# A two-layer decoder kernel: tile 1's last four heads sorted and chosen in two windows, and the order around the first gathered rows

## The reference

```python
q = (xc @ w_query).reshape(c, PEER_HEADS, 2, half)
scores = jnp.einsum('chpd,hpnd->chpn', q, sub_keys, preferred_element_type=jnp.float32)
s1, i1 = lax.top_k(scores[:, :, 0], PEER_TOPK)
s2, i2 = lax.top_k(scores[:, :, 1], PEER_TOPK)
cand_s = (s1[..., :, None] + s2[..., None, :]).reshape(c, PEER_HEADS, PEER_TOPK * PEER_TOPK)
cand_id = (i1[..., :, None] * PEER_NKEYS + i2[..., None, :]).reshape(c, PEER_HEADS, PEER_TOPK * PEER_TOPK)
top_s, top_j = lax.top_k(cand_s, PEER_TOPK)
ids = jnp.take_along_axis(cand_id, top_j, axis=-1)
gate = jax.nn.softmax(top_s, axis=-1)
u = expert_u[ids]
pre = jnp.einsum('chkd,cd->chk', u, xc, preferred_element_type=jnp.float32)
act = gate * jax.nn.gelu(pre, approximate=False)
return jnp.einsum('chk,chkd->cd', act.astype(expert_v.dtype), expert_v[ids])
```

## Time and profile before

| | us |
|---|---|
| median of three runs | 1544.27 |
| lowest, highest | 1544.26, 1545.46 |
| the profiled execution | 1546.54 |
| its span | 1544.8 |
| busy PE / DVE / ACT / POOL | 1133.4 / 1043.4 / 577.2 / 583.4 |
| bytes moved by DMA | 607.35 MB, mean 393 GB/s |

### The profile page before, as it was taken

How to read it: one execution, slowest core, us unless ns; L and a number is a source line. 1 busy time by engine, 2 the same in 40 slices (tenths; PEclk the granted TensorE clock), 3 DMA queues, 4 the chain that set the end, 5 groups by cost and what they waited for, 6 DMA issues and landing times.

```text
span 1544.8 us, 18402 instructions
## 1 busy us (share of the span) xinstructions
PE 1133.4 (73%) x6396; PEld 450.3 (29%) x6396; DVE 1043.4 (68%) x2678; ACT 577.2 (37%) x1802; POOL 583.4 (38%) x516
## 2 busy tenths in 40 slices
PE   8887776986568865778657887699566867666666
PEld 6653232451113522234112443245011311111112
DVE  3677987579996246667998537767799565454545
ACT  0415447333334145423334325733234343333332
POOL 0024444334544332434544333443444353333430
PEclk9999888897779967888687997899577986676668
DMA  9278999999999999999999999999999999999993
GB/s 360 99 317 366 412 408 376 386 408 418 421 420 411 418 417 419 420 405 396 421 421 407 417 418 421 395 398 417 420 421 420 369 422 422 421 421 422 421 421 156
DMA packets 90253, 607.35 MB, mean 393 GB/s; under 512 B 9904, under 2 KB 10416, under 8 KB 24624
## 3 DMA queue, kind: packets, MB, share of 16 engines
q0 software_dynamic: 73728, 536.90, 84.5%
q1 hardware_dynamic: 16272, 69.02, 11.2%
q10 hardware_dynamic: 160, 0.26, 0.1%
HBM read 605.09 MB, written 1.05 MB: 392 GB/s over the span
## 4 chain that ended last, share of the span: by engine, by line
DMA 35%; PE 27%; DVE 26%; ACT 5%; issue 5%; POOL 2%; SPq 0%; POOLq 0%; ACTq 0%; DVEq 0%
DMA ring<-in_rows,ids 34%; DVE ring L1314 12%; PE acc L578 10%; PE bank L902 3%; PE bank L981 2%; POOL ring L545 2%; PE bank L611 2%; PE bank L741 2%; PE bank L616 1%; DVE wb L1651 1%; PE bank L646 1%; DVE top_i L1645 1%; DVE y L1724 1%; DVE top_i L1660 1%; ACT diag L1071 1%
## 5 line engine op out<-in xcount | busy, mean ns | idle before, releaser
L545 POOL DMA_INDIRECT ring<-in_rows,ids x512 | 583.2, 1139 | 923.5 <-PE acc L578 758.6
L578 PE MATMUL acc<-ring,diag 64*64 64x512 f32 x3968 | 671.5, 786 | 311.4 <-ACT diag L1071 307.5
L1314 DVE CUSTOM_DVE_ANT_0 ring<-ring,xc 128x1024 f32<-128x1024 f32 x504 | 608.4, 1224 | 380.3 <-DMA ring<-in_rows,ids 369.7
L1062 ACT ACTIVATE gel<-pre 128x1 f32<-128x1 f32 x512 | 103.4, 202 | 782.4 <-DVE pre L1314 746.9
L578 PEld LDWEIGHTS acc<-ring,diag 64*64 64x64 f32 x3968 | 139.9, 160 | 782.4 <-ACT diag L1071 662.1
L1071 ACT ACTIVATE diag<-cst,act_w 128x64 f32<-128x64 f32 x512 | 178.1, 348 | 16.7
L1068 ACT ACTIVATE act_w<-gate,gel 128x1 f32<-128x1 f32 x512 | 150.7, 294 | 16.7
L902 PEld LDWEIGHTS bank<-hT,held 128*128 128x128 f32 x384 | 43.8, 192 | 10.9 <-issue 8.1
L902 PE MATMUL bank<-hT,held 128*128 128x128 f32 x384 | 46.1, 278 | 1.0 <-DVE hT L1353 1.0
L741 PE MATMUL bank<-wring,hT 128*128 128x512 f32 x96 | 44.2, 603 | 3.1 <-DVE hT L1356 3.1
L1314 DVE DVE_READ_ACCUMULATOR2_ANT pre<- 128x1 f32 x512 | 42.1, 82 | 0.0
(11 more groups left out here) (285 smaller groups left out, 1073.9 us busy)
## 6 DMA issues: line engine op xcount, KB each, us to landing
wring<-in_w_in SPq DMA_DIRECT2D x16, 978.0 KB
wring<-in_w_out SPq DMA_DIRECT2D x12, 1024.0 KB
wring<-in_w_gate SPq DMA_DIRECT2D x11, 1024.0 KB
held<-in_w_query SPq DMA_DIRECT2D x8, 1024.0 KB, 22.0
ring<-in_rows,ids POOLq DMA_INDIRECT x512
ring<-in_w_in SPq DMA_DIRECT2D x8, 978.0 KB, 15.7
held<-in_w_out SPq DMA_DIRECT2D x2, 1024.0 KB, 12.3
held_latent<-in_w_latent SPq DMA_DIRECT2D x2, 768.0 KB
```

The costliest lines, as they stand in the source:

```text
L545: pool.indirect_dma_start(out=ring[:, n % RING, :], out_offset=None, in_=rows, in_offset=bass.IndirectOffsetOnAxis(ap=index, axis=0),).the ...
L578: last = pe.matmul(acc[rows_of(c), r, :], diag[rows_of(r), j, :], ring[rows_of(r), j, D:][:, cols_of(c)], start=False, stop=True, skip_gro ...
L1062: act.activation(gel[:, j:j + 1], pre[:, j:j + 1], ACT.Gelu).then_inc(gelued, 1)
L1314: dve.tensor_tensor_reduce(out=u, in0=u, in1=x, scale=1.0, scalar=0.0, op0=ALU.mult, op1=ALU.add, accum_out=pre[:, j:j + 1]).then_inc(dott ...
```

## The change

It does five things.

1. SP issues slab 0 of `w_in` right behind x, ahead of the constants.
2. In tile 0's `rest`, `copy_group(1)` stands behind the squares and the reciprocal root.
3. `FIRST` is 1; `query_group(2)` stands two turns later in `choose(0, 1)`, and `keys_group(2)` with ACT's copy of the queries moves into `leave(1)`.
4. In window 0, chunks 2 and 3 of tile 1 (its heads 4 to 7) are only sorted, in two turns each. The sum of the window's numbers is 159.4 instead of 177.8. The other four turns of each chunk (`pick`) stand in window 1, in `front(2)`, between the eight input slabs. Window 1's own numbers are as they were.
5. Tile 1's gate is made in two halves: heads 0 to 3 in window 0, heads 4 to 7 in window 1. SP's load of `held_latent` waits for `latent_done`, no longer for `ids_ready`.

```diff
-FIRST = 3
+FIRST = 1
+NEAR = 2
...
 def window_turns(w):
 
     turns = HEAD + LATE_LEAVE + CHOOSE * 3 if w == 0 else EMBED
+    if w == 0:
+        return turns + HOPS_LATE + REST + CHOOSE * NEAR + CHOOSE[0:2] * (len(CHUNKS[1]) - NEAR) + [2]
...
             for c in range(len(CHUNKS[w + 1])):
-                parts["choose"](w + 1, c, turn)
+                if w == 0 and c >= NEAR:
+                    parts["sort"](w + 1, c, turn)
+                else:
+                    parts["choose"](w + 1, c, turn)
...
             load(h[:, 0, :], x[0:P, :], x_in[0])
+            load(ring[:, 0, 0:IN_W], w_in[0, 0:P, :], slab_in[0])
             load(cst[:], consts, consts_in)
...
                 turn()
+                if s == 1:
+                    keys_group(2)
                 next_of(normed)
...
                 for i in range(len(CHOOSE)):
-                    if (s, i) == (0, 1):
-                        if c == 2:
-                            next_of(latT_ready)
-                            next_of(cum_copied)
-                        if 1 <= c <= 3:
-                            query_group(c + 1, 0, KT // 4)
-                    if (s, i) == (0, 2) and 1 <= c <= 3:
-                        query_group(c + 1, KT // 4)
-                    if (s, i) == (0, 4) and 1 <= c <= 3:
+                    if (s, c, i) == (0, 2, 0):
+                        next_of(latT_ready)
+                        next_of(cum_copied)
+                    if s == 0 and 1 <= c <= 3:
+                        first = 3 if c == 1 else 1
+                        if i in (first, first + 1):
+                            query_group(c + 1, (i - first) * KT // 4, (i - first + 1) * KT // 4)
+                    if (s, i) == (0, 4) and 2 <= c <= 3:
                         keys_group(c + 1)
...
             def front(s, turn):
-                for _ in FRONT:
+                for n in range(len(FRONT)):
+                    if s == TILES and n in (4, 8):
+                        gate_exps(1, NEAR + n // 4 - 1)
                     turn()
...
                 copy_hT(gn[:, l, G_MIX:G_MIX + KT])
+                if s == TILES:
+                    for c in range(NEAR, len(CHUNKS[1])):
+                        pick(1, c, turn)
+                    return
...
                 if s == 0:
-                    copy_group(1, l)
                     next_of(group_in, 2)
                     for i in range(2):
                         squares(y[:, i * 256:(i + 1) * 256], i, wa[:, 512:768], 256)
                     rsqrt(2)
+                    copy_group(1, l)
                     next_of(row_gain_in, 16)
                     add_out(0, 0)
```

More of the change, by code:

```diff
@@ L121, in gate_heads, with gates_until @@
         return slice(*CHUNKS[s][c])
-    return slice(0, PH) if c == len(CHUNKS[s]) - 1 else None
+    if s == 1 and c == NEAR - 1:
+        return slice(0, CHUNKS[s][c][1])
+    if c == len(CHUNKS[s]) - 1:
+        return slice(CHUNKS[s][NEAR][0] if s == 1 else 0, PH)
+    return None
+def gates_until(s, k):
+    parts = [(i, gate_heads(i, c)) for i in range(STEPS) for c in range(len(CHUNKS[i]))]
+    ends = [(i, part.stop * TOPK) for i, part in parts if part]
+    return min(n + 1 for n, (i, end) in enumerate(ends) if i == s and end >= k)
 class Shares:
@@ L458, in _ @@
             load(posi[:], pos, small_in)
-            for k in range(KT):
+            for k in range(1, KT):
                 load(ring[:, k, 0:IN_W], w_in[0, k * P:(k + 1) * P, :], slab_in[k])
@@ L947, in choose, with sort @@
                         release(products(0, 1, weights(), bank[2:4]))
+                    turn()
+            def sort(s, c, turn):
+                for _ in range(2):
                     turn()
@@ L1048, in tail @@
                 totals(bank[0][:, 3:4], [slice(1, 2), slice(2, 3)], 5)
-            walk(Stream(experts, 2), {"front": front, "leave": leave, "rest": rest, "choose": choose, "embed": embed, "lift": lift,
+            walk(Stream(experts, 2), {"front": front, "leave": leave, "rest": rest, "choose": choose, "sort": sort, "embed": embed, "lift": lift,
                                        "begin": begin, "finish": lambda t: None, "ahead": ahead, "tail": tail})
@@ L1075, in __call__ @@
                     if b > a:
-                        act.wait_ge(gate_ready, len(CHUNKS[0]) + step if step else min(c + 1 for c, part in enumerate(CHUNKS[0]) if part[1] * TOPK >= b))
+                        act.wait_ge(gate_ready, gates_until(step, b))
                     Stream.__call__(self, step, a, b)
@@ L1129, in leave @@
                     act.wait_ge(slab_used, KT)
+                    copy_query(2)
                 turn()
@@ L1235, in choose, with gate_exps, sort @@
                                        ACT.Copy).then_inc(lift_copied, 1)
+            def gate_exps(s, c):
+                next_of(gate_in)
+                hs = gate_heads(s, c)
+                if hs:
+                    if (s, c) == (0, 0):
+                        next_of(scale_ready)
+                    act.activation(best_v[:, hs], best_v[:, hs], ACT.Exp,
+                                   scale=ffn_r[:, s % 2:s % 2 + 1]).then_inc(gate_exp, 1)
+            def sort(s, c, turn):
+                for _ in range(2):
+                    turn()
             def begin(w):
@@ L1289, in tail @@
                     act.dma_start(out[P:P + HALF_P, cols_of(c)], result_tail[rows_of(c), 0, :]).then_inc(stored, 16)
-            walk(GatedStream(experts, 1, first=FIRST), {"front": front, "leave": leave, "rest": rest, "choose": choose, "embed": embed, "lift": lift,
+            walk(GatedStream(experts, 1, first=FIRST), {"front": front, "leave": leave, "rest": rest, "choose": choose, "sort": sort, "embed": embed, "lift": lift,
                           "begin": begin, "finish": lambda t: None, "ahead": ahead, "tail": tail})
@@ L1675, in keys_next8, with sort, pick @@
                 next8(range(2 * a, 2 * z), top_v, top_i, lambda i: score(i, s), spare, s == 0)
+            def sort(s, c, turn):
+                keys_top8(s, c)
+                turn()
+                keys_next8(s, c)
+                turn()
             def choose(s, c, turn):
+                sort(s, c, turn)
+                pick(s, c, turn)
+            def pick(s, c, turn):
                 l, t = layer_tile(s)
```

18 lines of the change are left out of this document (4 added, 14 removed).

## The result

The changed kernel took 1532.95 us (median of six runs, 1530.67 to 1536.55) beside 1543.86 us for the kernel before on the same chip. The ratio is 0.9932, with a 95% interval of 0.9916 to 0.9948. A second set of six runs on another occasion gave 1531.10 us beside 1541.45, a ratio of 0.9919 (0.9894 to 0.9945). So the gain is 10.4 to 10.9 us by the medians, 10.5 to 12.5 by the ratios, where the forecast took off 14.2 us.

A forecast was written before the change was run, and what follows sets the result against it. Bound: bytes at full DMA rate plus holes where DMA moves less. Terms 0.8 + 2.0 + 4.8 + 1.2 + 5.4 = 14.2 us off 1544.3 gave 1530.1 us; own range 1527 to 1533.5, 8-in-10 range 1525 to 1539.

The forecast's parts named there:

- Slab 0 ahead: First projection: slab 0 issued ahead of the constants lets the third slab be used sooner; gain 0.8 us, ends 0 and 1.6.
- cannot overtake: Start loads: engines consume descriptors in ring order, so the constants queue behind slab 0, putting `gn` at 8.0 us.
- The copy: Tile 0's rest: copy_group(1) behind the root removes PE's 2.02 us wait for DVE's `y`; gain 2.0 us, low end 1.0.
- The restart: At 120 us: the ninth gather goes out at about 111.8, closing the 4.8 us hole; low end 2.5.
- the wait only moves: Rival: `leave(1)` waits for a late query copy and could reopen the whole 4.8 us; 1534.9 us, 12%.
- The hole at 190: Window 0: DMA sets the pace up to turn 27, so the 1.2 us hole closes; low end 0.
- `rest(1)`: Window 0: more rows per turn close the holes at 230, 240, 250 and 340; gain 5.4 us, ends 0 and 8.5.
- one more gather under way closes each: Step for 230, 240, 250 and 340: each hole, 1.0 to 2.0 us, is less than one row.
- The picks in window 1: Between tile 2's slabs: 17.8 us of DVE picks fill its waits for rows; cost 0, bad end 3 us.
- The slower rival: DVE becomes the bound between the slabs, adding picks, gate and ACT work; +7.3 us, 1551.6 us, 5%.
- Its dearer form: Counting a drain with each table load, 2.66 us per table switch, DVE bounding between slabs costs about 2.8 us more.
- the small holes stay: Rival: window 0's small holes could be fixed stalls as more rows load ACT too; gain 8.8 us less forecast, 1535.5 us, 23%.

The follow-up runs named there:

- slab_undone: The changed kernel with slab 0 of the input projection behind the constants again; one execution, 1533.88 us.
- start_only: The changed kernel without the split of tile 1's picks and gate, window 0's numbers summing to 177.8 again; 1533.14 us, ratio 0.9943 to the kernel before.
- split_only: The changed kernel with the four start edits undone (slab order, copy order, FIRST, query group), only the split kept; 1541.73 us, ratio 1.0000 to the kernel before.
- even_rows: The changed kernel with each sort's two turns weighing three times as much, so window 0's numbers sum to 177.8; 1534.46 us, ratio 0.9951 to the kernel before.
- hop_split: The changed kernel with three numbers of HOPS_LATE changed, sum as before, leaving fewer rows just ahead of PE's second weighing; 1530.53 us, ratio 0.9917 to the kernel before.

## Why the prediction was right, and where its sizes were off

Sign and range held; the forecast of 1530.1 us lies 1.0 and 2.9 us below the two medians, and the gain was 10.4 to 10.9 us instead of 14.2. That the second set comes so near is in part luck: the kernel before ran at 1541.45 us beside it, 2.8 us faster than the median that the forecast started from. By its terms:

- **Slab 0 ahead: 0.8 forecast, 0 measured.** The failed step took a wait of one execution for a wait of the kernel. A sign stood in the working itself: the third slab lagged 2.6 us behind its bytes and the constants did not the earlier trace rows; in `slab_undone` the same slab lags 0.8. The first gather at 92.7 instead of 93.8 looks better than forecast only because 96.61 was late. The same lateness would account for 1.7 of the 2.3 us by which before's profile lay above its median. `gn`, behind the slab, landed 5.8 us after its issue instead of 3.9, and PE waited no longer for what needs it (0.42 us ahead of the first slab, 0.44 in `slab_undone`); the transposes at 8.66 read `cst`, and `gn` is read only by DVE's copy behind them. That it came later agrees with what the Trainium skill (DMA: Bandwidth & Descriptors, Queues, rings and completion order) says of the order in which an engine takes descriptors. The prediction's "cannot overtake" goes further than that section, by which a later descriptor may finish its write before an earlier one; no run here shows one that did.
- **The copy: 2.0 forecast, 2.2 measured.** The mechanism is as told; PE's next product was not held up, so the low end didn't come.
- **The restart: 4.8 forecast, 4.8 measured** (the stretch from 120: 221 GB/s before, 424 now). No stretch near 120 is under 400. The ninth gather went out at 108.11, 3.7 us sooner than the 111.8 worked out. The working took the projection into `acc` at 106.4 from before's profile and didn't take off the 2.8 us that it gave to the start: PE began on `acc` at 105.86, 2.8 us sooner than worked out. And PE, idle for 1.62 us instead of 5.30, did this work in 1.09 us instead of 1.99. The rival "the wait only moves" fell: nothing is lost between 100 and 180. Unforeseen was that `FIRST` alone does it.
- **The hole at 190: 1.2 forecast, closed.** But the reason given (more rows per turn) is only one of two that do it: `start_only` closes it too, and `split_only` as well. Here the two halves overlap.
- **`rest(1)`: 5.4 forecast, 0.6 to 1.7 measured in five profiles and 3.9 in a sixth.** Before lost 9.5 us from 220 to 370; the changed kernel's two profiles lose 5.6 and 8.9, and the four with one edit taken back 7.8 to 8.9. By the ratios against `start_only` the split is worth 1.7 to 3.7. This is the term that was mis-sized. The step that failed is "one more gather under way closes each" with the rest of the order left as it is. The holes at 230, 240 and 340 did close. But more rows ahead of 270 delay tile 1's dense work behind them: the weighing L665 starts at 277.53, where `start_only` has it at 262.30. The hole near 280 grew by 1 us. And with the new numbers PE waits some 2.2 us instead of 0.56 ahead of the first weighing, the granted clock falls to 0.50 in most profiles, and a hole of 2 to 4 us opens at 260, which the working had no term for.
- **The picks in window 1: 0 forecast, 0 measured.** The stretch from 450 to 640 loses 1.8 us before and after. The slower rival fell. Its dearer form, with a drain at each table load, finds nothing in these traces either: a load takes 1.28 us and the next ACTIVATE follows at its end (273.36 and 274.65 above).

DVE's waits for rows, of the changed kernel from 470 to 550 us (tile 2's slabs, 80 us beside the 66 of the earlier trace rows) and from 211 to 350 us (beside the earlier trace rows):

```profile
DVE ring L1348 <- DMA ring<-in_rows,ids: 23.5, 13, 3.7
```

```profile
DVE ring L1348 <- DMA ring<-in_rows,ids: 32.1, 23, 2.7
```

The first shrank from 40.8 to 23.5 us (forecast some 22); the 66 us from 480, as long as the stretch before, have 18.1 in this profile and 25.4 in the second. The picks fill waits. As forecast, DVE also waits for rows ahead of 211 now: 2.6 us from 130 to 211, where before's profile has no such wait. The second grew from 26.9 to 32.1: in `rest(1)` DVE is not what holds up the rows, which is what `even_rows` says too.

With the measured terms the sum is 2.2 + 4.8 + 1.2 + (0.6 to 3.9) = 8.8 to 12.1 us, and 10.4 to 10.9 were measured (10.5 to 12.5 by the ratios). The rival "the small holes stay" (−8.8 us) had the size of this term nearly as well as the forecast: its 8.8 us are nearer to the medians' gain. Its mechanism was another: most of the small holes closed, and others opened. The size of the split's gain behind the start is not settled: the intervals of the ratios overlap, and the direct comparison leaves 0.3 to 5.5 us.

## What to carry to other kernels

- Where the time is the bytes plus the holes, count the lost DMA time stretch by stretch, and look for the one row that stands between an engine and dense work that doesn't need it. In `split_only`, closing the holes ahead of such a place only filled the next one (4.8 to 0.7 us lost ahead of 270, 3.2 to 8.3 behind it).
- A wait of 2 us for a transfer at the start of one profile should be held against the bytes ahead of it and against another execution with the same order. Here PE waited for the first slab in one profile of fourteen.
- The profile that happens to be taken can be the exception. One of ten had the dense chain at the higher clock level, and it was the first one of the changed kernel.
- Two edits can close the same hole. Their gains don't add, so each needs a kernel of its own.

## What the hardware showed that was not expected

- The same chain of matmuls in the same kernel ran at either clock level in different executions after the same idle span: 1.08, 1.02 and 1.02 us a piece at the granted clock 1.00, and 2.02, 1.92 and 1.76 us with the lower one. With an eight-slot ring this goes with 2.8 us of lost DMA time between these two profiles.
- A wait of 2.04 to 2.26 us ahead of the first weighing was followed by a slow one (2.91 to 3.68 us for 16 matmuls) in nine of ten profiles, a wait of 0.56 to 0.62 us in none of four (2.00 us).
- Behind the wait of 5.56 us PE's weighing took 3.67 us for 16 matmuls (L665 at 277.53), where the same form took 2.00 us at 256.36. The granted clock was 0.50 from 275 to 280 in that profile, and the dense work that everyone waits for paid for it. In `hop_split` the wait ahead of it is 2.52 us, and it takes 3.68 at a granted clock of 0.50 all the same.
- The slabs at the start of a launch arrived 1.6 to 1.8 us later in one execution than in others with the same order (13.2 us for 11.4 and 11.6), while the two loads of constants ahead of them did not.
